# A fused four-layer transformer kernel on one core: bias tables by one later product, first loads on one queue in order of need, and x's second half turned behind the first unit of weights

## The reference, cut to what matters

```python
h = rmsnorm(x, norm_mix[0])                                  # start of the first layer
b_gate, c_gate, u = jnp.split(h @ conv_w_in[0], 3, axis=-1)  # (256, 1024) @ (1024, 3072)
...
# second block, differential attention, 4 heads:
bucket = t5_bucket(k_pos[None, :] - q_pos[:, None])          # 32 buckets
bias = rel_bias[bucket].astype(jnp.float32).transpose(2, 0, 1)
s = jnp.einsum('bhcqd,bhcsd->bhcqs', qblk, kt).astype(jnp.float32) * scale + bias[None, :, None]
```

## Time and profile before

| what | value |
|---|---|
| median of three runs | 1266.78 us |
| the profiled execution's own time | 1267.27 us |
| its span in the trace | 1265.4 us |
| PE busy | 1239.2 us (98%) |
| DVE busy | 1001.6 us (79%) |
| ACT busy | 844.1 us (67%) |
| first product's first matmul | 14.48 us into the span |

### The profile page before, as it was taken

One profiled execution on the slowest core, in us unless ns is written; L12 is line 12 of the kernel. 1 busy time (PEld: TensorE's weight loads), 2 busy tenths in 40 slices (PEclk: granted clock), 3 DMA queues, 4 the chain that ended last, 5 costly groups with the idle time before them and its releaser, 6 DMA issues.

```text
span 1265.4 us, 18129 instructions
## 1 busy us (share of the span) xinstructions
PE 1239.2 (98%) x5924; PEld 1017.3 (80%) x5924; DVE 1001.6 (79%) x1397; ACT 844.1 (67%) x1218; POOL 39.1 (3%) x47
## 2 busy tenths in 40 slices
PE   7999999999999999999999999999999999999998
PEld 6888888888778787888788888888786877888887
DVE  6577555556977899999999999999999887765664
ACT  5666444446755788888888878888887587544442
POOL 0000000000100000000000000000100121000000
PEclk9999999999999999999999999999999999999999
DMA  9735555554233699999999999999996633455540
GB/s 356 275 133 215 190 193 175 190 199 166 68 133 134 252 379 373 378 348 365 368 379 360 353 360 379 375 356 366 376 422 264 238 146 115 163 176 195 178 155 34
DMA packets 48197, 325.22 MB, mean 257 GB/s; under 512 B 5417, under 2 KB 6705, under 8 KB 9873
## 3 DMA queue, kind: packets, MB, share of 16 engines
q1 hardware_dynamic: 44704, 316.40, 66.3%
q10 hardware_dynamic: 2752, 5.77, 1.2%
q0 software_dynamic: 688, 2.36, 0.5%
HBM read 318.74 MB, written 5.77 MB: 256 GB/s over the span
## 4 chain that ended last, share of the span: by engine, by line
PE 91%; DVE 4%; ACT 2%; issue 1%; DMA 0%; POOL 0%; SPq 0%; DVEq 0%; ACTq 0%
PE bank L431 26%; PE bank L433 25%; PE bank L432 25%; PE bank L1138 4%; PE bank L1139 2%; PE bank L495 2%; PE bank L845 1%; ACT wh L1196 1%; DVE wl L1827 1%; PE bank L467 1%; PE bank L700 1%; PE bank L1137 1%; PE bank L699 1%; DMA x<-x_dram 0%; DVE xt L1847 0%
## 5 line engine op out<-in xcount | busy, mean ns | idle before, releaser
L1827 DVE TENSOR_TENSOR wl<-raw,wh 128x1024 fp32r<-128x1024 f32 x598 | 714.7, 1219 | 178.0 <-ACT wh L1196 168.9
L1196 ACT ACTIVATE wh<-raw 128x1024 fp32r<-128x1024 f32 x598 | 630.6, 1058 | 273.1 <-PE bank L433 234.2
L431 PE MATMUL bank<-wh,xt 128*128 128x512 f32 (+2 forms) x1026 | 407.5, 397 | 5.7 <-DVE xt L1847 2.5
L433 PE MATMUL bank<-wh,xt 128*128 128x512 f32 (+2 forms) x1026 | 398.1, 388 | 0.0
L432 PE MATMUL bank<-wl,xt 128*128 128x512 f32 (+2 forms) x1026 | 397.5, 387 | 0.0
L431 PEld LDWEIGHTS bank<-wh,xt 128*128 128x128 f32 x1026 | 193.8, 189 | 44.3 <-DVE xt L1847 3.2
L433 PEld LDWEIGHTS bank<-wh,xt 128*128 128x128 f32 x1026 | 193.5, 189 | 40.6
L432 PEld LDWEIGHTS bank<-wl,xt 128*128 128x128 f32 x1026 | 194.1, 189 | 36.3
L431 PE MATMUL bank<-wh,hth 128*128 128x512 f32 x472 | 186.0, 394 | 1.1 <-DVE htl L1895 0.4
L433 PE MATMUL bank<-wh,htl 128*128 128x512 f32 x472 | 184.2, 390 | 0.0
L432 PE MATMUL bank<-wl,hth 128*128 128x512 f32 x472 | 183.8, 389 | 0.0
(11 more groups left out here) (304 smaller groups left out, 815.3 us busy)
## 6 DMA issues: line engine op xcount, KB each, us to landing
raw<-weights_dram SPq DMA_DIRECT2D x299, 1024.0 KB, 5.0
expert_results<-wide ACTq DMA_DIRECT2D x7, 512.0 KB
x<-x_dram SPq DMA_DIRECT2D x2, 512.0 KB, 7.7
wide<-bias_scratch ACTq DMA_DIRECT2D x8, 128.0 KB, 6.8
out_dram<-x SPq DMA_DIRECT2D x4, 256.0 KB, 2.0
fixed<-fixed_dram SPq DMA_DIRECT2D x1, 536.0 KB, 11.7
bias_scratch<-act ACTq DMA_DIRECT2D x2, 256.0 KB, 8.4
bias_scratch<-hbuf ACTq DMA_DIRECT2D x2, 256.0 KB, 15.1
```

Source lines behind the costliest of these rows:

```text
L431: mm(o, lh, wh[:, wi, sl], start=start, stop=False)
L433: return mm(o, ll, wh[:, wi, sl], start=False, stop=stop)
L1196: A(wh[:, c % SPLIT, 0:n], raw[:, (c // 2) % RAW, (c % 2) * UNIT:(c % 2) * UNIT + n], ACT.Copy).then_inc(hi_done, 1)
L1827: V.tensor_tensor(wl[:, c % SPLIT, 0:n], raw[:, (c // 2) % RAW, (c % 2) * UNIT:(c % 2) * UNIT + n], f32(wh[:, c % SPLIT, 0:n]), ALU.subtra ...
```

## The change

1. The bias table is one plain float32 matmul: the 32 x 4 bias values as stationary operand, the one-hot matrix as moving one, output 4 x 512 in one bank. It is issued behind the third product. DVE copies the 4 x 512 result once, behind its sixth unit and ahead of the angles. ACT issues one store that reads each of the four rows 128 times.
2. The identity moves from `fixed` to the front of `cols`. All first loads of SP are put in another order: `cols`, x's first half, the first unit of panel 0, x's second half, the second unit of panel 0, panel 1, bias values and one-hot, panel 2, `fixed`, panels 3 to 5. POOL issues its two loads only when panel 0 is there.
3. PE turns x's second half behind product 0 instead of ahead of it.

```diff
         @block.sync
         def _(sp):
+            halves = x_in.rearrange("(t p) d -> p t d", p=P)
+            sp.dma_start(cols[:, :], cols_in).then_inc(sem("cols_in"), 16)
+            sp.dma_start(x[:, :, 0:WIDE], halves[:, :, 0:WIDE]).then_inc(sem("x_in0"), 16)
+            sp.dma_start(raw[:, 0, 0:UNIT], weights[0][:, 0:UNIT]).then_inc(sem("first_in"), 16)
+            sp.dma_start(x[:, :, WIDE:D], halves[:, :, WIDE:D]).then_inc(sem("x_in1"), 16)
+            sp.dma_start(raw[:, 0, UNIT:2 * UNIT], weights[0][:, UNIT:2 * UNIT]).then_inc(raw_full[0], 16)
+            sp.dma_start(raw[:, 1, :], weights[1]).then_inc(raw_full[1], 16)
             sp.dma_start(relb[:, :], relb_in).then_inc(sem("rel_in"), 16)
             sp.dma_start(onehot, onehot_in).then_inc(sem("rel_in"), 16)
-            sp.dma_start(fixed[:, 0:P], fixed_in[:, 0:P]).then_inc(sem("cols_in"), 16)
...
+            sp.dma_start(raw[:, 2, :], weights[2]).then_inc(raw_full[2], 16)
+            sp.dma_start(fixed[:, :], fixed_in).then_inc(sem("fixed_in"), 16)
+            for p in range(3, RAW):
                 sp.dma_start(raw[:, p, :], weights[p]).then_inc(raw_full[p], 16)
...
         @block.gpsimd
+            g.memset(half[:, :], -0.5).then_inc(sem("half"), 1)
+            pool.wait_ge(sem("half"), 1)
+            pool.wait_ge(raw_full[0], 16)
             pool.dma_start(rows[:, :], rows_in.to_broadcast((P, NROWS))).then_inc(sem("pos_in"), 16)
             pool.dma_start(posi[:, :], pos_in).then_inc(sem("pos_in"), 16)
...
         @block.tensor
-            rel_bias(0)
-            rel_bias(1)
-            pe.wait_ge(sem("cols_in"), 32)
+            def rel_bias():
+
+                pe.wait_ge(sem("rel_in"), 32)
+                mm(bank[4][0:NB2, :], relb[:, :], onehot, start=True, stop=True).then_inc(sem("rel_T"), 1)
+
+            pe.wait_ge(sem("cols_in"), 16)
             turn_half("mix0", 0, 4)
-            rel_bias(2)
-            rel_bias(3)
-            turn_half("mix0", 1, 6)
...
-                chunk512(U_IN + 4 * j, 0, bank[2 * (j % 3):2 * (j % 3) + 2], normed("mix0") if j == 0 else None)
+                chunk512(U_IN + 4 * j, 0, bank[2 * (j % 3):2 * (j % 3) + 2], normed("mix0") if j == 0 else None,
+                         {0: lambda: turn_half("mix0", 1, 6), 2: rel_bias} if j == 0 else {})
...
         @block.scalar
-            for h in range(NB2):
-                sc.wait_ge(sem("rel_c"), h + 1)
-                sc.dma_start(scratch[h * P:(h + 1) * P, :], rel_rows[h]).then_inc(sem("rel_st"), 16)
+            sc.wait_ge(sem("rel_c"), 1)
+            sc.dma_start(scratch[0:NB2 * P, :].rearrange("(h p) n -> h p n", p=P),
+                         rel_rows[:, None, :].to_broadcast((NB2, P, WIDE))).then_inc(sem("rel_st"), 16)
...
         @block.vector
                 split_lo(c, 0)
-                if c == 1:
-                    rel_copy(2)
-                    rel_copy(3)
             for c in range(4, SPLIT):
                 split_lo(c, 0)
+            dv.wait_ge(sem("rel_T"), 1)
+            V.tensor_copy(rel_rows, bank[4][0:NB2, :]).then_inc(sem("rel_c"), 1)
```

More of the change, by code:

```diff
@@ L90 @@
 _at = 0
-for _name, _n in (("mix0", 8), ("ffn0", 8), ("mix1", 8), ("ffn1", 8), ("attn2", 8), ("mlp2", 8), ("qa", 3), ("kva", 2),
+for _name, _n in (("ident", P), ("mix0", 8), ("ffn0", 8), ("mix1", 8), ("ffn1", 8), ("attn2", 8), ("mlp2", 8), ("qa", 3), ("kva", 2),
                   ("qn", 1), ("kn", 1), ("conv", 24), ("bq", 1), ("bk", 1), ("sub", 1), ("router", 64)):
@@ L105 @@
 _at = 0
-for _name, _n in (("ident", 128), ("mask", 384), ("ctab", 128), ("stab", 128), ("freq", 32), ("iota", 8),
+for _name, _n in (("mask", 384), ("ctab", 128), ("stab", 128), ("freq", 32), ("iota", 8),
                   ("before", 128), ("slots", 128), ("every", 128), ("fold", 8)):
@@ L189, in build @@
         by_expert = results[0:(NE - 1) * P, :].rearrange("(e p) n -> e p n", p=P)
-        ident = fixed[:, FIXED["ident"]:FIXED["ident"] + P]
+        ident = cols[:, COLS["ident"]:COLS["ident"] + P]
         maskt = fixed[:, FIXED["mask"]:FIXED["mask"] + 384]
         onehot = ebuf[0:BUCKETS, 0, :]
-        picked = hth[0:BUCKETS, 0:2, :]
-        relh, rell = (v[0:BUCKETS, 2:4, :].rearrange("p a (h n) -> p (a h) n", h=2) for v in (hth, htl))
-        rel_rows = (act[:, 0, 3072:3584], act[:, 1, 3072:3584], hbuf[:, 0, :], hbuf[:, 1, :])
+        rel_rows = act[0:NB2, 0, 3072:3584]
         NORMS = ("mix0", "ffn0", "mix1", "ffn1", "attn2", "mlp2")
@@ L1190, in split_hi @@
             def split_hi(c, i):
-                sc.wait_ge(raw_full[(c // 2) % RAW], 16 * (c // ROUND + 1) + 16 * i)
+                if isinstance(i, int) and c + ROUND * i == 0:
+                    sc.wait_ge(sem("first_in"), 16)
+                else:
+                    sc.wait_ge(raw_full[(c // 2) % RAW], 16 * (c // ROUND + 1) + 16 * i)
                 if c >= SPLIT:
@@ L1311, in _ @@
             A(stat[:, 0:1], half[:, 0:1], ACT.Copy)
[L1312 removed]
+            sc.wait_ge(sem("cols_in"), 16)
             for c in range(4):
@@ L1623, in _ @@
             squares("attn2", 1)
-            sc.wait_ge(sem("rel_st"), 16 * NB2)
+            sc.wait_ge(sem("rel_st"), 16)
             for h in range(NB2):
@@ L2872 @@
     cols = np.concatenate([
-        column(w["norm_mix"][0]), column(w["norm_ffn"][0]), column(w["norm_mix"][1]), column(w["norm_ffn"][1]),
+        np.eye(P, dtype=np.float32), column(w["norm_mix"][0]), column(w["norm_ffn"][0]), column(w["norm_mix"][1]), column(w["norm_ffn"][1]),
         column(w["attn_norm_g_2"][0]), column(w["mlp_norm_g_2"][0]), column(w["mla_q_a_norm"][0]),
```

34 lines of the change are left out of this document (4 added, 30 removed).

## The result

The changed kernel takes 1279.37 us (median of four runs, 1278.69 to 1280.27) against 1266.85 for the kernel before, measured beside it. The ratio is 1.0102, with a 95% interval of 1.0089 to 1.0115: slower by 12.5 us. I had forecast 1265.3, no change. The profiled execution took 1278.69 us.

A forecast was written before the change was run, and what follows sets the result against it. PE, busy 98% of the span, was taken as the bound. Product 6 at N + 16.4 = 31.4 us in place of 32.86 saves 1.5 us: 1266.78 - 1.5 = 1265.3 us, counted as no change; range 1263.4 to 1267.2.

The forecast's parts named there:

- first transposes of x: Start of the kernel: x's first half, now SP's second load, is there at 4.5 us, before at 8.85.
- product 0: PE's first product: starts 4.9 us after x's first half lands, at 9.4 us, 5.1 us earlier than before.
- N: ACT may take a piece of x's second half once six of its eight transposes end: 15.0 us, before 14.44.
- bias matmul and the pause ahead of the next product: New matmul on PE among products 2 to 5: 0.4 to 0.9 us, hidden in PE's wait for unit 6.
- DVE's bias copy ends: DVE copies the bias result behind units 3 to 5, which end at N + 7.5: done at N + 8.1.
- sine: Starts when the chain of angles, 4.6 us behind the bias copy, is done: N + 12.7.
- sine, store and split, up to product 6: Sine, store of zeros and split of unit 6 on ACT and DVE take 3.7 us as before, to N + 16.4.
- product 6: First product on a unit not split at once: starts at 31.4 us in place of 32.86, after PE waits 1.4.
- Unit 0's weights are in time: First unit's weights, 512 KB, land 1.3 us behind x's first half and do not delay product 0.
- product 0 wholly at the lower clock: Rival: N at 16.2, product 6 at 32.6, gain only 0.3 us, 1266.5 us; chance 0.14.
- The table store holds ACT's queue: Rival: the zeros' store waits for the four-engine table store until 34.8; product 6 at 37.2, 1271.1 us; chance 0.07.
- no row shows an issue that long: Argument against the table store rival: in the rows the zeros' store issue took 1.28 us, far from seven.

The follow-up runs named there:

- the zeros ahead: The changed kernel with the store of zeros issued ahead of the one table store: 1267.59 us, ratio 1.0014.
- the table through DRAM: The changed kernel with table rows stored once, spread DRAM to DRAM behind the third chunk, zeros' store first, copy behind the angles: 1268.70 us, ratio 1.0009.

## Why the prediction was wrong

The steps in the order of the prediction, N being the moment at which ACT takes x's third piece:

| step | forecast | measured |
|---|---|---|
| first transposes of x | 4.5 | 4.96 |
| product 0 | 9.4 | 10.18 |
| N | 15.0 | 16.33 |
| bias matmul and the pause ahead of the next product | up to 0.9 | 0.95 (22.42 to 23.37) |
| DVE's bias copy ends | N + 8.1 | N + 7.8 |
| sine | N + 12.7 | N + 12.35 |
| sine, store and split, up to product 6 | 3.7 | 14.3 |
| product 6 | 31.4 | 42.98 |

**The start.** x came 0.5 us later than forecast. "Unit 0's weights are in time" was wrong by a little: they landed at 7.69 (1.66 + 6.03), ACT waited 0.31 us, and DVE's low part began at 8.81. The two make the 0.8 us in product 0. The other 0.5 of N is the clock: all twelve matmuls of product 0 took 0.43 us, which was the rival "product 0 wholly at the lower clock", with N = 16.2. That N came so near is partly luck: product 0 began 0.8 us later than in that rival, and from its end to ACT's piece passed 0.9 us, not 1.7. The Trainium skill's page TensorE: Matmul & The Clock Gate (Part 1: The HAM clock gate) says that the number of slow matmuls at the start differs from run to run. The traces agree: in the nine profiled executions with this same start, product 0 took 4.5 to 5.3 us. Eight of them turned x's second half between 14.98 and 16.00 us, landing times of the weights included, and the ninth, whose weights were late, at 17.16. So the start did wander, by up to 1 us, far less than what was lost here.

**The step that failed** is "Sine, store and the split of unit 6 took from 27.48 to 31.1, 3.7". It carried the zeros' store at its old 1.28 us, behind a table store of a new form. The rival "The table store holds ACT's queue" named the mechanism, the place and the instructions behind it, and I gave it 0.07. Its sum was too low at 1271.1. Four of its terms were off:

- The price of a packet. I took 88 ns from the earlier trace rows, a mean over all transfers of ACT's queue in the whole kernel. From 34 to 40 us it is 0.232 x 16 x 6 us of engine time for 77 packets, 289 ns.
- The point of release. I had ACT held until the store was through, at 34.8; it was let go at 40.5 with 84 packets an engine left, and the store ran on until 70.1. This error points the other way.
- The start. I had the packets run from the issue on. The store was issued at 24.19, and ACT's queue shows no packet before 28.3.
- The clock. A PE that waits 11 us comes back at 1.2 GHz: 1.7 us more, which the sum lacked.

How far luck can carry such a sum shows in the run with rows on 0, 4, 8 and 12, which has the price that I assumed (84 ns). There ACT was let go at 34.7 and product 6 came at 37.2, the rival's own 34.8 and 37.2, only because the late start and the early release cancel.

I also argued "no row shows an issue that long". No row could: the old table stores, 128 rows each, had eight packets for an engine if all 16 shared them. The lack of a row was a lack of a case, and I took it for evidence.

Without the hold it is the rival of the slow product 0 that stands (32.6, a gain of 0.3), not the main forecast: with the zeros ahead, product 6 came at 32.3 and the mark 0.5 us early. The supply was sized well: there, ACT took x's third piece at 16.89 and the low part of unit 6 was ready at 31.8, which with the 1.3 us of the zeros' issue makes N + 16.2 against N + 16.4. But PE had no wait there, where I had forecast 1.4 us: with the zeros' issue still in the chain it would have been some 0.8 (an estimate, 33.1 against 32.3), since the slow product 0 made PE itself late. With the table through DRAM product 6 came at 31.3 and the mark 1.5 us early, the forecast's numbers by another way: the copy and the zeros were off the supply's chain, and PE was the bound. In time neither gain is seen: the medians are 1.3 and 1.8 us above before, ratios 1.0014 and 1.0009, so no change, as predicted, but on the slower side.

**Why 26 GB/s.** From partitions 0 to 3 the store moved 26 GB/s with 3.7 engines busy and 27 with 14.6 busy; from 0, 32, 64 and 96 it moved 49, from 0, 4, 8 and 12 it moved 103. The Trainium skill's page SBUF — State Buffer (Door 1: The DMA port swizzle) gives a map that fits these: SBUF has 16 ports for DMA of some 27 GB/s each, partitions 0 to 3 and 32 to 35 share one, 64 to 67 and 96 to 99 another, 4, 8 and 12 lie on three more. That gives 27, 54 and 109, an estimate from the page; the traces agree within a tenth. The Trainium skill's page DMA: Bandwidth & Descriptors (Rules for kernel authors), which the prediction cited for four engines, held too (3.7 busy), but from partitions 0 to 3 the rows' place was the narrower of the two: the same four engines moved 103 GB/s from elsewhere.

## What to carry to other kernels

A store that repeats a few rows reads them over and over from the partitions where they lie: spread what is read over partitions on different ports, or repeat it from DRAM, and price it by that, not by the bytes. Issue it so that nothing urgent stands behind it: here the order of two stores was worth 12 us at the mark, a store four times as fast 5. Count the packets that each DMA engine gets, and put no short, urgent DMA, nor work queued behind one, on the same queue behind a store that leaves each engine a hundred of them. When a change puts an instruction in a form that the trace has never shown, the old rows bound it poorly, and a rival on it deserves more than 0.07.

## What the runs showed of the hardware

- **ACT's queue holds the engine.** With 128 packets for each of four engines, the next DMA issued on ACT took 11.82, 11.79, 7.38 and 5.81 us, and was let go each time with 80 to 86 packets an engine left. With 64 each it took 0.80, and with 32 each on 16 engines 2.20. Compute instructions behind it on ACT wait as long.
- **A slow store from one port blocks the others' engines.** On 16 engines it kept them 91% busy at 27 GB/s, and weights arrived 16 us late; on four engines it left the weights alone. Four engines were then the better choice.
- **The clock dips in places that the edits don't touch.** Leaving out the last few us, where the clock is down in every profile, before shows two dips of 3.4 us; the other kernels had none to four, of 3.4 to 10.2 us, some of them behind a long wait of PE. Ten runs of one kernel spread over 8 us, while four of the change lay within 1.6. I did not find what decides whether a dip comes; that stays open, and with it why the two kernels that lead at the mark don't lead in the median.
